# Storing and combining the two plain MLP slabs in a hybrid encoder kernel: pairs 2 to 5 instead of the last pair, with a new order of the first pair

## The reference, cut to what matters

```python
h = rmsnorm(x, g_mlp[l])
x = x + jnp.square(jax.nn.relu(h @ w_up[l])) @ w_down[l]     # 1024 -> 4096 -> 1024
```

## Time and profile before

| | |
|---|---|
| median of 3 runs | 2516.36 us |
| profiled execution | 2515.44 us |
| its span, first to last instruction | 2513.6 us |
| mean granted TensorE clock | 0.984 |
| busy: PE, DVE, ACT, POOL | 95%, 68%, 45%, 10% |
| pairs in layer 0 and layer 1 (first product to last) | about 633 to 943 us, 1869 to 2178 us |
| packets' time as a share of the 16 DMA engines | q1 (SP's queue) 35.1% |

### The profile page before, as it was taken

One profiled execution on the slowest core, in us unless ns is written; L12 is line 12 of the kernel. 1 busy time (PEld: TensorE's weight loads), 2 busy tenths in 40 slices (PEclk: granted clock), 3 DMA queues, 4 the chain that ended last, 5 costly groups with the idle time before them and its releaser, 6 DMA issues.

```text
span 2513.6 us, 32774 instructions
## 1 busy us (share of the span) xinstructions
PE 2385.5 (95%) x11857; PEld 1935.6 (77%) x11857; DVE 1702.0 (68%) x3128; ACT 1125.1 (45%) x2008; POOL 260.1 (10%) x286
## 2 busy tenths in 40 slices
PE   8999999899899989999999999998999999799998
PEld 6877777678688877888888777776777888688886
DVE  5555566666777768888636556666577777697872
ACT  5554444544444433333436544454454444333334
POOL 1111111123000000000221101121220000000002
PEclk9999999999999999999999999998999999899999
DMA  5201010211344467868330000102114444787753
GB/s 181 68 26 26 18 35 26 68 51 51 122 143 150 148 215 248 270 190 264 126 93 26 26 26 26 26 26 71 56 43 159 144 154 162 234 273 238 222 182 101
DMA packets 289928, 296.06 MB, mean 118 GB/s; under 512 B 19510, under 2 KB 236640, under 8 KB 289512
## 3 DMA queue, kind: packets, MB, share of 16 engines
q1 hardware_dynamic: 283968, 278.21, 35.1%
q10 hardware_dynamic: 5800, 15.75, 1.6%
HBM read 212.10 MB, written 81.82 MB: 117 GB/s over the span
## 4 chain that ended last, share of the span: by engine, by line
PE 79%; DVE 8%; issue 4%; ACT 4%; DMA 2%; DVEq 2%; SPq 0%; ACTq 0%; POOL 0%; POOLq 0%
PE ps L1896 24%; PE ps L2163 20%; PE ps L2215 8%; PE ps L2217 8%; PE ps L2216 8%; PE ps L2029 3%; PE ps L1976 3%; PE ps L2059 2%; PE ps L2049 1%; DVE probs L1401 1%; ACT pt_both L1040 1%; ACT probs L1022 1%; DVE probs L1429 1%; PE ps L2061 1%; DMA b_saved<-v_tile 1%
## 5 line engine op out<-in xcount | busy, mean ns | idle before, releaser
L2215 PE MATMUL ps<-b_hi,d_hi 128*128 128x512 f32 x896 | 351.1, 392 | 11.0 <-DVE d_lo L1693 11.0
L2216 PE MATMUL ps<-b_lo,d_hi 128*128 128x512 f32 x896 | 350.0, 391 | 0.0
L1896 PE MATMUL ps<-wide_hi,w_hi 128*128 128x512 f32 x1024 | 337.2, 411 | 13.4 <-DVE c_parts L1340 5.5
L2217 PE MATMUL ps<-b_hi,d_lo 128*128 128x512 f32 x896 | 349.8, 390 | 0.0
L1896 PE MATMUL ps<-wide_lo,w_hi 128*128 128x512 f32 x1024 | 319.7, 394 | 0.0
L1896 PE MATMUL ps<-wide_hi,w_lo 128*128 128x512 f32 x1024 | 318.5, 392 | 0.0
L1452 DVE TENSOR_TENSOR pt_both<-ps,pt_both 128x512 fp32r<-128x512 f32 (+3 forms) x216 | 126.4, 585 | 223.0 <-ACT pt_both L1040 222.2
L1144 ACT ACTIVATE d_hi<-d_raw 128x1024 fp32r<-128x1024 f32 x112 | 118.2, 1057 | 335.7 <-PE ps L2217 110.0
L1040 ACT ACTIVATE pt_both<-ps 128x512 fp32r<-128x512 f32 (+3 forms) x216 | 110.5, 512 | 338.5 <-PE ps L2029 338.1
L1022 ACT ACTIVATE probs<-probs,neg_max,slope 128x256 f32<-128x256 f32 (+7 forms) x256 | 202.3, 791 | 95.1 <-DVE neg_max L1416 75.0
L865 POOL TENSOR_TENSOR w_lo<-w_raw,w_hi 128x256 fp32r<-128x256 f32 x216 | 158.0, 762 | 831.0 <-ACT w_hi L915 831.0
(11 more groups left out here) (206 smaller groups left out, 4474.3 us busy)
## 6 DMA issues: line engine op xcount, KB each, us to landing
b_raw<-b_saved SPq DMA_DIRECT2D x112, 512.0 KB, 6.7
d_raw<-in_w_down_dram SPq DMA_DIRECT2D x112, 512.0 KB, 6.2
a_raw<-in_w_up_dram SPq DMA_DIRECT2D x60, 512.0 KB, 4.2
b_saved<-c_rows SPq DMA_DIRECT2D x120, 256.0 KB, 4.4
w_raw<-in_w_in_dram SPq DMA_DIRECT2D x92, 256.0 KB, 3.3
b_saved<-far SPq DMA_DIRECT2D x32, 512.0 KB, 4.3
w_raw<-in_w_out_dram SPq DMA_DIRECT2D x36, 256.0 KB, 3.0
x_saved<-xt ACTq DMA_DIRECT2D x16, 512.0 KB, 3.0
```

The source lines that it names most:

```text
L1896: mm = T.matmul(ps[p][:, bass.ts(t, BANK)], w, h[:, bass.ts(t, BANK)], start=(start and n == 0), stop=(stop and n == 2))
L2215: T.matmul(out, w0, b0, start=first, stop=False)
L2216: T.matmul(out, w0, b1, start=False, stop=False)
L2217: mm = T.matmul(out, w1, b0, start=False, stop=last)
```

## The change

The four combinations of the plain slabs are made one by one, each in place in the tile `far`, in pairs 2, 3, 4 and 5. `store_ring` now sends each slab as two halves, three of them to their final place in `b_saved` and one to `plain_saved`; `load_plain(p, n)` fetches two quarters into `far`, `make_plain_t(p)` combines them, `store_plain(p)` sends the result. T4 is written over C21 as before, but in pair 13 into a tile of the weight sums and in pair 14 over C12. P4 of the first pair has its split operand in `far`, so it waits for no ring store. On ACT, DVE and SP the order of the first two pairs is new. On SP and DVE the order of the last pair is new too, as follows from the combinations' going. What PE computes, and its order, is the same.

```diff
+        far_hi = place("far_hi", [P, NC // 2, P], far_at, F32R)
+        far_lo = place("far_lo", [P, NC // 2, P], far_at + 2 * KB, F32R)
...
+        def t4_tile(l, n):
+            if n == NP - 2:
+                return s_sum[l][0][:].rearrange("p c m -> p (c m)")
+            return c_block[l][C12 if n == NP - 1 else C21]
...
         def free_slot(engine, l, n, i):
-            if n:
+            if (n, i) == (0, P4):
+                return
+            if (n, i) == (1, P4):
+                engine.wait_ge(ring_stored[1], 32 * (l + 1))
+            elif n:
                 engine.wait_ge(product, products(l, n - 1, i))
...
                 def store_ring(m):
                     sp.wait_ge(u_squared, (NPLAIN + 4 * NP) * l + m + 1)
-                    sp.dma_start(plain_saved[m], ring[m][:]).then_inc(ring_stored[m], 16)
+                    for dst, at in ((kept(P2 if m else P1, -1), 0), (kept(P3, -1) if m else plain_saved, H)):
+                        sp.dma_start(dst, ring[m][:, at:at + H]).then_inc(ring_stored[m], 16)
...
+                def load_plain(p, n):
+                    sp.wait_ge(t13_stored, 16 * (NP * l + n))
+                    if 4 * l + p:
+                        sp.wait_ge(v_stored, 16 * (4 * l + p))
                     for m in range(NPLAIN):
+                        sp.wait_ge(ring_stored[m], 32 * (l + 1))
+                    first = kept((P1, P3, P3, P2)[p], -1)
+                    second = (plain_saved, plain_saved, kept(P5, -1), kept(P6, -1))[p]
+                    for src, at in ((first, 0), (second, H)):
+                        sp.dma_start(far[:, at:at + H], src).then_inc(v_loaded, 16)
+
+                def store_plain(p):
+                    sp.wait_ge(v_made, 4 * l + p + 1)
+                    sp.dma_start(kept((P5, P7, P6, P4)[p], -1), far[:, 0:H]).then_inc(v_stored, 16)
...
+                store_ring(0)
                 load_a(1, 0)
-                for n in range(NP - 1):
-                    load_a(n + 1, 1)
-                    if n:
+                load_a(1, 1)
+                store_ring(1)
+                store_block(0, C11)
+                store_block(0, C22)
+                for n in range(1, NP - 1):
+                    if n == 1:
+                        store_t13(0)
+                        store_block(0, C21)
+                        store_t2(0)
+                        load_a(2, 0)
+                        load_a(2, 1)
+                    else:
+                        load_a(n + 1, 1)
                         store_t13(n - 1)
                         store_block(n - 1, C21)
                         store_t2(n - 1)
-                        store_t4(n - 1)
+                    if 2 <= n < 6:
+                        load_plain(n - 2, n)
+                    store_t4(n - 1)
                     if n + 2 < NP:
                         load_a(n + 2, 0)
+                    if 2 <= n < 6:
+                        store_plain(n - 2)
                     store_block(n, C11)
                     store_block(n, C22)
-                load_plain()
+                load_d(0, "A21")
                 store_t13(NP - 2)
                 store_block(NP - 2, C21)
                 store_t2(NP - 2)
+                store_t4(NP - 2)
                 load_b(0, 0)
                 load_d(0, "A11")
                 load_b(0, 1)
-                store_plain()
-                store_t4(NP - 2)
                 load_b(0, 2)
-                store_plain_t()
                 load_b(0, 3)
...
```

`load_a(2, 0)` also waits now for `sum_a(1, 2)`. ACT's new order of the first pairs:

```diff
+                t_high(T2)
+                t_high(T3)
                 a_high(0, P5)
-                t_high(T2)
                 a_high(0, P6)
                 a_high(0, P2)
                 copy_out(0, P1)
-                t_high(T3)
+                t_high(T4)
                 square_ring(0)
                 a_high(0, P7)
                 copy_out(0, P5)
-                t_high(T4)
+                copy_out(0, P6)
                 a_high(0, P3)
-                copy_out(0, P6)
+                a_high(0, P4)
+                a_high(1, P1)
                 square_ring(1)
-                a_high(0, P4)
+                a_high(1, P5)
+                square_block(0, C11)
+                a_high(1, P6)
+                square_block(0, C22)
+                square_block(0, C12)
+                square_block(0, C21)
+                copy_out(1, P1)
+                for i in (P2, P7, P3, P4):
+                    a_high(1, i)
...
```

DVE, the first pairs, in its new order (all of it up to the loop, which now begins at n = 1), and the last pair, where `make_plain_t()` ahead of `add_block` is gone and the second product's splits come after C22:

```diff
+                t_low(T3)
+                a_low(0, P7)
                 V.drain()
                 sum_a(0, 3)
...
+                a_low(0, P3)
+                a_low(0, P4)
+                t_low(T4)
+                add_block(0, C11)
+                add_block(0, C22)
                 hidden(1)
+                a_low(1, P1)
+                sum_a(1, 0)
+                V.drain()
+                sum_a(1, 1)
+                rectify(0, C11)
+                a_low(1, P5)
+                rectify(0, C22)
+                add_block(0, C12)
+                V.drain()
+                rectify(0, C12)
+                rectify(0, C21)
+                make_t13(0)
+                a_low(1, P6)
+                a_low(1, P2)
+                make_t2(0)
+                sum_a(1, 2)
+                V.drain()
+                sum_a(1, 3)
+                a_low(1, P7)
+                a_low(1, P3)
+                a_low(1, P4)
...
-                    if not ahead:
-                        make_plain_t()
                     add_block(n, C11)
...
                     rectify(n, C22)
...
+                    if 2 <= n < 6:
+                        make_plain_t(n - 2)
                     if ahead:
                         a_low(n + 1, P7)
                     else:
-                        b_low(0, 2)
-                        b_low(0, 3)
+                        d_low(0)
+                        for j in range(4):
+                            b_low(0, j)
                         d_sums(0)
...
+                        d_low(1)
                         b_low(0, 4)
                         b_low(0, 5)
                     rectify(n, C21)
...
-                d_low(1)
                 make_t13(NP - 1)
                 make_t2(NP - 1)
+                make_t4(NP - 1)
                 b_low(0, 6)
                 b_low(0, 7)
-                V.drain()
-                make_t4(NP - 1)
```

More of the change, by code:

```diff
@@ L794, in _ @@
                 load_d(1, "A11")
+                store_block(NP - 1, C11)
                 store_block(NP - 1, C22)
@@ L1215, in _ @@
                 square_block(NP - 1, C22)
+                d_high(1)
                 square_block(NP - 1, C12)
@@ L1746, in _ @@
                 sum_a(0, 2)
+                t_low(T3)
+                a_low(0, P7)
                 V.drain()
                 sum_a(0, 3)
-                t_low(T3)
-                a_low(0, P7)
-                hidden(1)
-                a_low(0, P3)
-                t_low(T4)
-                a_low(0, P4)
-                for n in range(NP):
+                a_low(0, P3)
[3 more added lines that the diff above has]
+                add_block(0, C22)
+                hidden(1)
+                a_low(1, P1)
[19 more added lines that the diff above has]
+                a_low(1, P4)
+                for n in range(1, NP):
                     ahead = n + 1 < NP
-                    if n:
+                    if n > 1:
                         make_t13(n - 1)
                         make_t2(n - 1)
-                    if ahead and n:
+                    if ahead:
                         a_low(n + 1, P1)
@@ L1765, in _ @@
                         a_low(n + 1, P5)
-                    if n:
-                        V.drain()
-                        make_t4(n - 1)
-                    if not ahead:
-                        make_plain_t()
+                    make_t4(n - 1)
                     add_block(n, C11)
-                    if ahead and n:
+                    if ahead:
                         sum_a(n + 1, 2)
                     V.drain()
-                    if ahead and n:
+                    if ahead:
                         sum_a(n + 1, 3)
                     rectify(n, C11)
-                    if ahead and n:
+                    if ahead:
                         a_low(n + 1, P6)
                         a_low(n + 1, P2)
-                    elif not ahead:
-                        d_low(0)
-                        b_low(0, 0)
-                        b_low(0, 1)
                     add_block(n, C22)
@@ L1787, in _ @@
                     rectify(n, C22)
-                    if ahead and n == 0:
-                        a_low(n + 1, P1)
-                        sum_a(n + 1, 0)
-                        V.drain()
-                        sum_a(n + 1, 1)
-                        a_low(n + 1, P5)
-                        sum_a(n + 1, 2)
-                        V.drain()
-                        sum_a(n + 1, 3)
-                        a_low(n + 1, P6)
-                        a_low(n + 1, P2)
```

(2 more changed lines are left out.)

104 lines of the change are left out of this document (39 added, 65 removed).

## The result

| | before | after |
|---|---|---|
| median of six runs each | 2516.91 us (2515.53 to 2518.69) | 2494.78 us (2490.63 to 2498.89) |
| ratio | 1 | 0.9914, 95% interval 0.9902 to 0.9926 |
| profiled execution | 2515.44 us | 2490.63 us |
| its span, mean granted clock | 2513.6 us, 0.984 | 2488.5 us, 0.989 |

The change makes the kernel 0.86% faster. The forecast was 2495.4 us, with 2488 to 2506 as its range; the sign and the mechanism hold, and the main term to a fifth (22.0 us against 18.6 in the profile); the slow stretch at the end and the sum of the first pairs do not.

The account below looks back on a forecast made before the run. PE sets the pace in pairs 2 to 13; its largest waits, for DVE's add_block and d_low, trace to stores at the last pair. 2 x (9.3 + 1.6) - 0.8 - 0 = 21.0 us off 2516.36: 2495.4 us, range 2488 to 2506.

Parts of the forecast that it names:

- the main term: From P3's end in pair 14 to the third unit's start: 9.3 us gained in each layer.
- the slow stretch at the end: Third unit: its wait falls to 2.6 us, so no half-rate stretch follows, 1.6 us more gained in each layer.
- the sum of the first pairs: Pairs 0 and 1, both layers: 1.9 + 0.5 - 3.2 = -0.8 us, a net loss.
- The last pair: Pair 14: add_block no longer held by a store, P4 starts at 930.3, the 8.3 us wait gone.
- I take 951.5: Start of the third unit in layer 0, 951.5 us against 960.84 before.
- The rival had 4 us a layer: Second product: loads d_raw or b_raw become the next bound, 4 us late each layer, 2503.4 us; chance 0.12.
- First pairs: P4 of pair 1 at 677.7 against 679.63 in layer 0: 1.9 us gained, 0.5 in layer 1.
- 1.6 lost in each layer: P4 of pair 1: its own wait of 3.9 us brings a slow-clock stretch, costing 1.6 us a layer.
- the clock gives it back: Five waits of 2.0 to 3.9 us a layer remain; slow stretches after the others too cost 12.8, 2508.2 us; chance 0.12.
- Pairs 2 to 5: 0: Added loads, combinations and stores cost nothing there, up to 5.0 us of store landing; ends 0 and 0.5 per pair.
- The 24 us that the rule could have cost: Six more fixed DMA parts in both layers, if all stood on the path: 24 us, time 2519.
- The slower rival: Pairs 2 to 5: store_plain landing after 7.95 us delays make_t13 and P6, 36.4 us, 2531.8 us; store late chance 0.10.

Follow-up runs that it names:

- experiment 3: Kernel after, with ACT taking copy_out of P5 and P6 of pair 1 ahead of a_high(2, P1): 2497.89 us, ratio 0.9933.
- experiment 2: Kernel after, with the old order of pairs 0 and 1 and P4's slot as it was, so the plain slabs alone: 2497.53 us, ratio 0.9928.
- experiments 6: Kernel after, without load_plain, make_plain_t and store_plain in pairs 2 to 5, their places in HBM filled once with weights: 2502.38 us, ratio 0.9941.
- experiment 7: Kernel after, with store_plain storing each piece five times and make_t13 waiting for all five: 2497.05 us, ratio 0.9936.
- experiment 4: Kernel after, with T4 of pairs 13 and 14 written over C21 as in pairs 0 to 12: 2503.97 us, ratio 0.9952.

## Why the prediction was right, and where it was off

**The last pair** is right in its mechanism. `add_block` no longer stands behind a store: DVE starts it at 923.34 (C11) and 926.06 (C22), where the forecast had it done by 926.5 and 928.6. The forecast kept the old time of P3's end, 930.3; it was 928.51, as the first pairs gained more. Counted from P3's end, `d_high(0)` begins 2.0 us before it (forecast 2.3), and the second side of unit 0 starts 10.4 us behind it (forecast 10.1) after a wait of 2.12 us (forecast 2.0).

**"I take 951.5" is the term that was mis-sized.** The forecast's two ends were 951.1 to 952.7 by the landing of a load and 949.4 by DVE's own queue. The queue decided: 949.4 is 19.1 us after P3's end, and the third unit came after 19.3 and 19.8 us, not the 21.2 taken. The load's 8.0 us were the median of loads issued into a full queue; this one followed 6.8 us without an issue and took 4.3. That makes 3.4 us more for the two layers than the forecast's 18.6.

**"I take no slow stretch" at the end was wrong in its reason.** A stretch of 7 or 8 half-rate matmuls falls in each layer behind the wait of 2.12 and 2.56 us at unit 0's second side, though the forecast read from the earlier trace rows that 2.19 and 2.46 us went without one. It had looked at the first matmul behind a wait only. The stretch can begin some matmuls later, and did so in the kernel before, layer 1, pair 0, behind a wait of 2.12 us (PE's timeline of the kernel before):

```profile
1890.69 0.47 PE L2163 MATMUL ps<-t_hi,a_hi 128*128 128x512 f32 x1 [2.12 <-DVE c_rows L1619]
...
1891.93 0.39 PE L2163 MATMUL ps<-t_hi,a_lo 128*128 128x512 f32 x1
1892.16 0.59 PE L2163 MATMUL ps<-t_hi,a_hi 128*128 128x512 f32 x1
1892.54 0.63 PE L2163 MATMUL ps<-t_lo,a_hi 128*128 128x512 f32 x1
```

In layer 0 it cost little: behind it the third unit waited only 0.35 us for DVE, so unit 0 at full clock would have waited for the same `d_low`. The third unit itself is at full rate, as forecast. But the 1.6 us that this was to give back per layer do not appear: the later units wait 1.45 and 0.46 us for `d_low` where before one waited 0.37, and the stretch from the third unit to the end of the stage is 0.5 us longer.

**What comes next** is a load of the second product after all, with a small price. The chain of waits in the kernel after, layer 0:

```profile
944.90 6.60 DMA b_raw<-b_saved
951.52 1.07 ACT b_hi L1167
```

It is the first load behind the last pair's own stores, and through `d_low`, queued behind its split, it holds the fourth unit for 1.45 us (1.06 in layer 1). The rival had 4 us a layer for this; it is a fourth to a third of that.

**First pairs.** P4 of pair 1 was due 59.1 us after the mark (677.7), and came at 57.95 to 58.5 in all eighteen layers of the nine profiles taken with this order (experiment 3 has another on ACT and isn't counted). `a_low(1, P4)` ended at 664.5, as forecast (664.6), and `sum_a(2, 0)` started 4.0 us later; the chain from there to P4 took 8.1. The waits ahead of P7 and P4 are there, 2.75 and 3.23 us. That the first of them costs nothing, experiment 3 shows.

The price of the clock at this place, "1.6 lost in each layer", is right as a size and wrong as a certainty. P5 of pair 2, the second product after P4, starts at about 63.7 us after the mark in nine of those eighteen layers (63.6 to 64.1), at about 65.1 in eight (64.9 to 65.3), and at 66.7 in one. In the first case the half-rate matmuls fell in P7, ahead of a wait that absorbs them; in the second on P4, with 65.1 - 63.7 = 1.4 us lost; in the last from P4 into the next product, 14 matmuls long. Their mean is 64.5. The old order (the kernel before and experiment 2) stands at 65.2 to 66.6 in four layers, mean 65.7. So these two pairs gain 1.1 us a layer on average, 2.3 us in all, where the forecast had -0.8.

The Trainium skill (TensorE: Matmul & The Clock Gate, the part on the clock gate) says that the number of slow matmuls varies from run to run of one kernel, as the chip's monitor doesn't start anew with the kernel. The traces agree: in the two profiles of the kernel after, P4 stands at 58.0 to 58.3 us, and P5 of pair 2 at 63.8, 65.1, 65.2 or 66.7, with 7 to 14 slow matmuls. The rival "the clock gives it back" charged five waits; the profile has one stretch at pair 1's waits and one in the last pair of each layer, and of these the former costs in layer 0 alone.

**Pairs 2 to 5: 0** is right, by experiments 6 and 7, and safer than thought: the bound was 5.0 us of landing, and the store lands in 2.3. The 3.8 us of the earlier trace rows were the median of two kinds of store, 2.0 and 4.5 us, and `store_plain` is of the first: like T4's store before, it is issued with nothing close ahead of it. The Trainium skill (DMA: Bandwidth & Descriptors, section on the anatomy of one DMA) would give 256 KB, as an estimate, 2.0 us fixed and 0.6 for the bytes, on GpSimd's path; SP's stores from `far` took 2.3 and T4's 2.0. No lone store of another size stands here, so these runs can't tell a fixed part from the bytes' share. The 24 us that the rule could have cost are not seen, as the work in pairs 2 to 5 has no price on PE. The slower rival, a store landing after 7.6 us, fell with it; that a late landing there does reach PE is shown by experiment 7.

**The sum** came near by misses that partly cancel. Up to P3's end in pair 14 the change gained 4.1 us more than forecast, from there to the third unit 3.4 more, and behind the third unit 4.3 less: 24.2 against 21.0. That the medians agree to 0.6 us, with single runs spread over 8 us, is luck in part.

## What to carry to other kernels

Take a DMA's landing time from transfers that meet the same load on the queue: a median over a burst overstated a lone load by 3.7 us, and here the engine's own queue was the bound. A buffer whose reuse waits for a store is dearest where the engine that waits has the next phase's work queued behind it: two combinations written to another place at the end of each layer carry some 11 of the 24 us in the profile. When two profiles are compared, cut the stage at the place from which the kernels differ: of 4.6 us between two of them 3.3 lay ahead of it. And a wait can be removed without gain when a later one absorbs it; look at where the next wait ends before pricing it.

## What the runs showed of the hardware

Half-rate stretches of TensorE are not tied to the length of one wait: 2.12 us was followed by one, 2.75 us in layer 0 was not, and 3.02 us at the same place in layer 1 was. They came 6 to 14 matmuls long in the kernel after and the experiments on it (18 once, in experiment 4), and could begin up to six matmuls behind the wait. The same program's MLP stages differ by 2.8 us between two profiles; in layer 1 of the second a stretch of 14 at pair 1 accounts for 2.9 us (63.8 to 66.7), and other places gave some of it back.

Stores of 256 KB from SP landed in 2.0 us (T4, 11 stores, in both kernels), 2.3 (from `far`), 4.4 to 4.5 (C blocks) and 4.7 (T2, in both kernels), all between 690 and 900 us. T4's store is issued at 692.00 with no other issue of SP within 3.3 us on either side; T2's at 704.70, behind a load and a store of 512 KB and one store of 256 KB in the 2.1 us before. So transfers of one size, in one stretch with one busy share of the DMA engines (0.48), land after 2.0 or 4.7 us: the share does not tell the landing. That what stands close ahead in the queue does is inferred from the order of the issues; no run here varied it alone.
